# One core, trn2: the delta-rule stage of a two-layer decoder step written in another order

## Chip, cores, metric

One Trainium2 chip (trn2), one core. The metric is the device time of one call in microseconds (us), the median of three runs.

## The reference, cut to what matters

The program is one step of a decoder with two layers, over 256 prompt tokens and 8 sample tokens at once (T = 264 columns). Each layer adds four gated branches to x, then a mixture of experts. The change lies in the third branch, the gated delta rule with a state of 64 x 64 per head (4 heads):

```
qkv, conv_new = causal_conv(qkv_raw, conv0, w)        # 4 taps
qkv = silu(qkv);  gq, gk, gv = split(qkv)
gq = l2norm(gq) * 64 ** -0.5;  gk = l2norm(gk)
beta = sigmoid(b_raw)
g = -exp(a_log) * softplus(alpha_raw + dt_bias)
# per chunk, state s: 
gcum = cumsum(g);  decay = exp(tril(gcum_t - gcum_s))
lmat = eye + strict(beta * (k k^T) * decay)
u = solve(lmat, beta * v) - solve(lmat, beta * exp(gcum) * k) s
o = exp(gcum) * (q s) + ((q k^T) * decay) u
s = exp(g_last) * s + (exp(g_last - gcum) * u)^T k
c_out = rmsnorm(o) * silu(z_gate)
```

For the prompt s starts at zero; each of the 8 sample tokens has a state of its own and takes one step. The branch's gate is sigmoid of a column block of the input projection; there are 32 such blocks of 128 columns ("gate tiles") in a layer.

## The kernel before, in words

A layer is a chain of stages with a barrier of all engines behind each: `project`, `mla_prompt`, `mla_decode`, `gdn`, `memory`, `tail` (experts). All activations lie in on-chip memory with channels on partitions. Every engine has its own program, written by hand; semaphores order them, and an engine that waits holds up all that stands behind on it. There is no scheduler: the order in the code is the order on the engine.

The gate tiles are filler work for PE (TensorE). `gate_load` (L486) brings 512 KB of weights into one of two buffers `wf` on SP's DMA queue, `gate_multiply` (L494) runs 8 products of 128 x 128 by 264 columns on them, `gate_copy` (L507) takes the sum out of its PSUM bank on ACT. A load into a buffer waits until the product before it on that buffer is done. Before the change 8 tiles are multiplied in `mla_prompt`, 16 in `gdn`, 8 in `memory`.

`gdn` (L1297) handles the prompt as two chunks of 128 tokens (j = 0, 1). It has three parts.

- Head. DVE runs the convolution (L1558 to L1566), ACT its SiLU (L1510); DVE squares q and k (L1573), PE sums the squares per head with a block matrix (L1384), ACT takes four roots, DVE the reciprocal of 1,056 columns (L1582) and two multiplies (L1583, L1585). Then DVE and ACT make beta and the decay from short vectors of 12 columns (L1576 to L1599), DVE spreads them to `rep` (L1603), PE turns them into rows (L1400, L1402) and makes k k^T and k q^T (L1408), DVE the masked and decayed matrices AT, PT, MT (L1613 to L1625, once per chunk).
- Levels. The triangular inverse is made by doubling: after a level 0 (L1419) a loop of six levels, each with two products that hang on each other (L1426, then L1432 and L1435), ACT's copy between (L1539), and DVE's updates of X and XT (L1642, L1644). One gate tile stands at the end of each level.
- End. k and v are turned (L1444, L1448), the sample tokens' rows are spread, then per chunk: k s (L1464), q s (L1471), u (L1475), o (L1481), the new state (L1487), with DVE between them (L1700 to L1723). The sample tokens' state update (L1670 to L1733) stands between these DVE steps. Last the norm of o (L1728, L1498, L1548, L1736) and the product with the gate (L1737).

The first transfers that SP issues in `gdn` are the convolution's history `buf`, three small stores of runs of 12 or 32 bytes and the sample state; the stage's first gate load stands behind them.

## Time and profile before

| | us |
|---|---|
| three runs | 1571.75, 1576.78, 1569.12; median 1571.75 |
| profiled execution, its own time | 1580.17 |
| its span, first to last instruction | 1578.4 |
| PE busy in the span | 1331.3 (84%) |
| DVE, ACT, POOL busy | 722.7, 327.1, 183.0 |
| mean granted clock of PE | 0.92 of full |

The profile has one row for each group of instructions: when the group starts, how long it is busy, its engine and line, what it writes and reads, its count, and in brackets how long the engine stood idle before it and what ended that. PEclk in a window is the granted share of PE's full clock (1.00 is 2.4 GHz, 0.50 is 1.2 GHz). Matmuls in float32 have two records each. A row of windows has the stretch and its length, the busy time (and records) of PE, PEld (weight loads), DVE, ACT and POOL, then PEclk, the DMA engines' share and GB/s.

### The profile page before, as it was taken

How to read it: one execution, taken by the hardware profiler on the slowest of the kernel's cores; microseconds unless marked ns; L12 is line 12 of the kernel's file. 1: busy time of each engine (PE TensorE's matmuls, PEld its weight loads, DVE VectorE, ACT ScalarE, POOL GpSimd, SP SyncE). 2: the span in 40 equal slices, each digit the busy share in tenths (PEclk: the TensorE clock that was granted, in tenths of full speed). 3: DMA queues.
4: the chain of work that ended last, by engine and by line, in shares of the span. 5: the costliest groups of instructions: out<-in, count | busy, mean ns of one | idle time of the engine just before them, and what ended most of it. 6: DMA issues, size and time to landing. Idle time of an engine off the chain costs nothing. (4 is left out here: it accounts for less than half of the span.)

```text
span 1578.4 us, 23156 instructions
## 1 busy us (share of the span) xinstructions
PE 1331.3 (84%) x8264; PEld 921.3 (58%) x8264; DVE 722.7 (46%) x1485; ACT 327.1 (21%) x628; POOL 183.0 (12%) x192
## 2 busy tenths in 40 slices
PE   5988978977889799978779889789697897999876
PEld 3866756966466544433249666679564675444332
DVE  4664757365453512222246647463744525222222
ACT  0212613111121221111011235221102212121110
POOL 0050000000000243331000400000000003333210
PEclk9998989978899789999989989899798897899998
DMA  5372022126147189999734610311261482899995
GB/s 192 121 240 67 0 51 74 54 80 230 65 137 283 69 338 408 409 409 408 289 119 160 213 53 1 71 54 56 91 240 41 137 333 98 338 408 409 409 409 237
DMA packets 89962, 307.95 MB, mean 195 GB/s; under 512 B 16368, under 2 KB 19200, under 8 KB 88192
## 3 DMA queue, kind: packets, MB, share of 16 engines
q1 hardware_dynamic: 86784, 296.11, 50.1%
q0 software_dynamic: 3072, 10.49, 1.9%
q8 instruction: 59, 0.97, 0.3%
q14 instruction: 47, 0.39, 0.1%
HBM read 403.24 MB, written 3.98 MB: 258 GB/s over the span
## 5 line engine op out<-in xcount | busy, mean ns | idle before, releaser
L502 PE MATMUL bank<-hT,wf 128*128 128x264 f32 x1024 | 252.1, 405 | 34.4 <-PEq L205 19.5
L502 PEld LDWEIGHTS bank<-hT,wf 128*128 128x128 f32 x1024 | 202.4, 201 | 76.8 <-issue 23.0
L2032 PE MATMUL bank<-tail_wbase,tail_scr 128*32 128x512 f32 x1024 | 186.4, 604 | 21.2 <-DMA tail_wbase<-in_w_gu 21.2
L2032 PE MATMUL bank<-tail_wover,tail_scr 128*32 128x512 f32 x512 | 185.4, 601 | 4.5 <-DMA tail_wbase<-in_w_gu 4.5
L2366 DVE TENSOR_TENSOR xT<-xT,bank 128x264 f32<-128x264 f32 x192 | 73.7, 426 | 148.2 <-PE bank L2061 145.5
L2048 PE MATMUL bank<-tail_wbase,tail_acT 128*32 128x512 f32 x512 | 94.9, 622 | 22.2 <-DMA tail_wbase<-in_w_d 14.7
L2008 PEld LDWEIGHTS bank<-tail_G,tail_hTM 88*128 88x128 f32 x528 | 70.3, 196 | 68.5 <-issue 64.1
L2048 PE MATMUL bank<-tail_wover,tail_acT 128*32 128x512 f32 x256 | 94.6, 613 | 7.6 <-ACT tail_acT L2210 3.8
L1881 POOL MEMSET tail_wover<- 128x3072 f32 x2 | 5.3, 2659 | 805.5 <-PE bank L1970 805.5
L270 DVE TENSOR_TENSOR tail_Y<-bank,tail_Y 128x512 fp32r<-128x512 f32 x48 | 30.9, 686 | 146.1 <-ACT tail_Y L2215 146.1
L2008 PE MATMUL bank<-tail_G,tail_hTM 88*128 88x256 f32 x528 | 87.8, 305 | 2.8 <-ACT tail_scr L2160 2.8
L2032 PEld LDWEIGHTS bank<-tail_wbase,tail_scr 128*32 128x32 f32 x1024 | 42.6, 110 | 77.2 <-issue 73.2
L2160 ACT COPY tail_scr<-bank 128x256 f32<-128x256 f32 x96 | 35.8, 373 | 200.4 <-PE bank L2008 174.5
L1935 PE MATMUL bank<-brT,wbr 128*128 128x264 f32 x256 | 65.8, 420 | 9.7 <-DMA wbr<-in_w_br 5.2
L1911 POOL TENSOR_SCALAR tail_Gt<-tail_rows,cst 128x528 f32<-128x528 f32 x24 | 38.5, 1605 | 291.6 <-PE bank L2061 286.9
L1970 PE MATMUL bank<-hT,tail_wo 128*128 128x264 f32 x256 | 65.6, 408 | 4.7 <-DVE tail_last L2244 4.7
L2061 PE MATMUL bank<-tail_Q,tail_Y 128*128 128x264 f32 x384 | 65.5, 295 | 2.9 <-DVE tail_Y L270 2.8
L276 PE MATMUL bank<-proj_hsp,proj_wsp 128*128 128x264 f32 x224 | 64.6, 288 | 2.2 <-DVE proj_wsp L270 2.1
L1935 PEld LDWEIGHTS bank<-brT,wbr 128*128 128x128 f32 x256 | 52.5, 208 | 22.3 <-issue 12.2
L2061 PEld LDWEIGHTS bank<-tail_Q,tail_Y 128*128 128x128 f32 x384 | 53.8, 191 | 18.9 <-issue 11.7
L277 PE MATMUL bank<-proj_hsp,proj_wsp 128*128 128x264 f32 x224 | 63.5, 283 | 0.0
L278 PE MATMUL bank<-proj_hsp,proj_wsp 128*128 128x264 f32 x224 | 63.4, 283 | 0.0
(517 smaller groups left out, 2165.4 us busy)
## 6 DMA issues: line engine op xcount, KB each, us to landing
tail_wbase<-in_w_gu SPq DMA_DIRECT2D x256, 512.0 KB, 15.0
tail_wbase<-in_w_d SPq DMA_DIRECT2D x128, 512.0 KB, 15.1
tail_wover<-in_w_gu ACTq DMA_DIRECT2D x128, 512.0 KB
wf<-in_w_gate SPq DMA_DIRECT2D x64, 512.0 KB, 3.7
tail_wover<-in_w_d ACTq DMA_DIRECT2D x64, 512.0 KB
proj_wfm<-in_w_fm SPq DMA_DIRECT2D x28, 512.0 KB, 3.6
wbr<-in_w_br SPq DMA_DIRECT2D x16, 512.0 KB, 3.8
tail_wo<-in_w_out SPq DMA_DIRECT2D x16, 512.0 KB, 6.5
```

Source lines behind the costliest of these rows:

```text
L276: pe.matmul(out, wh, xh, start=start, stop=False)
L277: pe.matmul(out, wh, xl, start=False, stop=False)
L278: return pe.matmul(out, wl, xh, start=False, stop=stop)
L502: mm = pe.matmul(E["bank"][to][:, 0:T], F["wf"][slot][:, k, :], E["hT"][:, k, :], start=k == 0, stop=k == KT - 1)
L1911: nc.gpsimd.tensor_scalar(Gt[:], rows[:], C("slot")[:, q:q + 1], None, ALU.is_equal)\
L1935: mm = pe.matmul(bank[4 * s + b][:, 0:T], w[s][:, 2 * b + k, :], brT[:, 2 * b + k, :], start=k == 0, stop=k == 1)
L1970: mm = pe.matmul(bank[i][:, 0:T], wo[i][:, k, :], mixT[:, k, :], start=k == 0, stop=k == KT - 1)
L2008: mm = pe.matmul(bank[to][:, 0:GCOLS], h[0:n, c, P * k:P * k + P], G[g % 2][0:n, c, :], start=part == 0 and c == 0, stop=part == 1 and c == 2)
L2032: mm = pe.matmul(bank[0][W * p:W * p + W, :], HS[q // GROUP % 2][:, k, at + W * p:at + W * p + W], w[p][:, 512 * (k % 2):512 * (k % 2) + 5 ...
L2048: mm = pe.matmul(bank[2 + half][W * p:W * p + W, :], acT[:, f, W * p:W * p + W], w[p][:, 512 * half:512 * half + 512], start=f == 0, stop= ...
L2061: mm = pe.matmul(bank[4 + n % 3][:, 0:T], Y[part][:, P * d:P * d + P], Q[:, q % 2, :], start=part == 0, stop=part == 1)
L2366: tt(x, x, bank[4 + n % 3][:, 0:T], ALU.add).then_inc(S("x_ready"), 1)
```

## The change

- Gate tiles: tile 8 is multiplied in `mla_decode`, in front of the wait for the softmax's exponential, into PSUM bank 4, and kept in a new buffer `g8`; `gdn` copies it to its place and keeps 15 tiles. Of these, five stand in the head, one between level 0 and level 1, one behind each of levels 1 and 2, two behind each of levels 3, 4 and 5, none behind level 6, and the last one at the stage's very end.
- SP: the gate loads go first; the small stores are issued behind the load of the last gate tile. The last load for the next stage waits for the last gate product.
- Head: the short vectors of the decay come first on DVE; the convolution runs on four tiles (q, k), then the samples' taps as 4 instructions in place of 18, then on the other two; SiLU likewise in two pieces. The sums of squares go to 32 rows per tile, one root and one reciprocal of 264 columns stand for four; PE spreads the result with a selecting matrix `pick`, and DVE multiplies from PSUM.
- k and v are turned before level 0. Level 6 leaves out the update of X, which nobody reads.
- The steps of the sample state stand one after each level's MT on DVE (`between`).
- End: chunk 0 has no k s, q s and no decayed old state; the parts of o for chunk 1 add up in one bank; the norm of o is made in two halves.

```diff
-            for i in range(2):
-                gate_load(sp, S, A, l, F, i, MLA_TILES + i)
-            for i in range(2):
-                sp.wait_ge(S(f"gw{i}_loaded"), 16)
+            gate_load(sp, S, A, l, F, 0, MLA_TILES)
+            gate_load(sp, S, A, l, F, 1, MLA_TILES + 2)
+            gate_load(sp, S, A, l, F, 0, MLA_TILES + 1, used=1)
+            sp.wait_ge(S("gw0_loaded"), 32)
+            sp.wait_ge(S("gw1_loaded"), 16)
...
+            pe.wait_ge(S("rT_read"), 1)
+            gate_multiply(pe, S, E, F, 0, 1, 4)
             pe.wait_ge(S("exp_done"), 1)
...
+            pe.wait_ge(S("gate_copied"), 1)
             pe.transpose(bank[4][:, 0:P], lat[:], ident).then_inc(S("latT_done"), 1)
...
+            act.wait_ge(S("gate_done"), 1)
+            nc.scalar.copy(F["g8"][:], bank[4][:, 0:T]).then_inc(S("gate_copied"), 1)
...
         def _(sp):
             sp.dma_start(buf[:], A["sconv"][l]).then_inc(S("buf_loaded"), 16)
+            for r in range(2, 8):
+                gate_load(sp, S, A, l, F, r % 2, FIRST + r, used=r - 1)
+                if r == 3:
+                    sp.dma_start(st[:], A["sgdn"][l]).then_inc(S("state_loaded"), 16)
+            with sp.Fori(0, 3) as k:
+                for i in range(2):
+                    gate_load(sp, S, A, l, F, i, FIRST + 8 + i + 2 * k, used=2 * k + (7 + i))
+            sp.dma_start(F["memT"][:], A["memT"]).then_inc(S("mem_loaded"), 16)
+            gate_load(sp, S, A, l, F, 0, FIRST + 14, used=13)
+
             sp.dma_start(A["o_conv"][l], raw[:, :, NP_TOK - 3:NP_TOK]).then_inc(S("stored"), 16)
             sp.dma_start(A["o_convs"][l, :, :, 2, :], raw[:, :, NP_TOK:T]).then_inc(S("stored"), 16)
...
-            for r in range(2, 9):
-                gate_load(sp, S, A, l, F, r % 2, MLA_TILES + r, used=r - 1)
-            with sp.Fori(1, 7) as k:
-                gate_load(sp, S, A, l, F, 1, MLA_TILES + 8 + k, used=k + 8)
-            gate_load(sp, S, A, l, F, 0, MLA_TILES + 15, used=9)
-
-            sp.dma_start(F["memT"][:], A["memT"]).then_inc(S("mem_loaded"), 16)
-            gate_load(sp, S, A, l, F, 1, MLA_TILES + GDN_TILES + 1, used=15)
-            gate_load(sp, S, A, l, F, 0, MLA_TILES + GDN_TILES, used=16)
+            gate_load(sp, S, A, l, F, 1, MLA_TILES + GDN_TILES + 1, used=14)
             sp.wait_ge(S("state_s_ready"), 1)
             sp.dma_start(A["o_gdns"][l], st[:]).then_inc(S("stored"), 16)
-            sp.wait_ge(S("state_ready"), 8)
+            gate_load(sp, S, A, l, F, 0, MLA_TILES + GDN_TILES, used=15)
+            sp.wait_ge(S("state_ready"), 2)
...
-            for t in range(4):
-                mm = pe.matmul(bank[t][:, 0:T], C("blk"), sq[:, t, :], start=True, stop=True)
...
+            gates(0, 1, 2)
+            pe.wait_ge(S("sq_ready"), 1)
+            for t in range(4):
+                mm = pe.matmul(bank[2][32 * t:32 * t + 32, 0:T], C("blk")[:, 48:80], sq[:, t, :], start=True,
+                               stop=True)
+            mm.then_inc(S("ss_done"), 1)
+            gates(3)
+            pe.wait_ge(S("gb_ready"), 3)
...
+            pe.wait_ge(S("rinv_ready"), 1)
+            for t in range(4):
+                if t >= 2:
+                    pe.wait_ge(S("qk_ready"), t - 1)
+                pe.matmul(bank[2 + t % 2][:, 0:T], C("pick")[32 * t:32 * t + 32], rinv[32 * t:32 * t + 32, :],
+                          start=True, stop=True).then_inc(S("spread"), 1)
+            pe.wait_ge(S("rep_ready"), 4)
+            rows(0)
+            pe.wait_ge(S("qk_ready"), 4)
+            kq(0)
+            gates(4)
+            pe.wait_ge(S("G_ready"), 2)
+            rows(1)
+            pe.wait_ge(S("gate_copied"), 5)
+            kq(1)
+            pe.wait_ge(S("silu_done"), 2)
+            pe.wait_ge(S("bB_done"), 1)
+            turn(0)
+            level_zero(0)
+            pe.wait_ge(S("bB_done"), 2)
+            turn(1)
+            level_zero(1)
+            gate_multiply(pe, S, E, F, 1, 2, 7)
+            pe.wait_ge(S("kv_ready"), 2)
+            level(1)
+            gate_multiply(pe, S, E, F, 0, 3, 7, 6)
...
+            level(2)
+            gate_multiply(pe, S, E, F, 1, 3, 7, 7)
...
+            pe.wait_ge(S("rs_read"), 1)
+            with pe.Fori(3, LAST) as k:
+                level(k)
+                gate_multiply(pe, S, E, F, 0, k + 1, 7, 2 * k + 2)
+                gate_multiply(pe, S, E, F, 1, k + 1, 3, 2 * k + 2)
+            level(LAST, last=True)
+
+            pe.wait_ge(S("gate_copied"), 14)
+            pe.wait_ge(S("oX_ready"), 1)
+            for t in range(2):
+                mm = pe.matmul(bank[7][:, N * t:N * t + N], oX[:, 8 * t:8 * t + 8, :].rearrange("p a b -> p (a b)"),
+                               C("seln"), start=True, stop=True)
+            mm.then_inc(S("os_done"), 1)
+
...
+            pe.wait_ge(S("x0_ready"), 2 * LAST + 1)
+            values(0)
+            pe.wait_ge(S("x1_ready"), 2 * LAST + 1)
+            pe.wait_ge(S("us_ready"), 1)
+            state(0)
+            pe.wait_ge(S("u_ready"), 1)
...
+            pe.wait_ge(S("state_ready"), 1)
+            for h in range(H):
+                o, a = HD * (h % 2), h // 2
+                mm = pe.matmul(bank[h % 2][:, HD * a:HD * a + HD], y[o:o + HD, 2 + a, REST][:, 0:P],
+                               ST[o:o + HD, a, :], start=True, stop=True)
+            mm.then_inc(S("kS_done"), 1)
...
+                mm = pe.matmul(bank[4][:, P * t:P * t + P], C("blk"), osq[:, t, FIRST_HALF], start=True, stop=True)
+            mm.then_inc(S("oss_done"), 1)
+            values(1)
+            pe.wait_ge(S("u_ready"), 2)
...
+            pe.wait_ge(S("osq_ready"), 2)
+            n = T - P
             for t in range(2):
-                mm = pe.matmul(bank[t][:, 0:T], C("blk"), osq[:, t, :], start=True, stop=True)
+                mm = pe.matmul(bank[0][:, n * t:n * t + n], C("blk"), osq[:, t, REST], start=True, stop=True)
             mm.then_inc(S("oss_done"), 1)
+            gate_multiply(pe, S, E, F, 0, 7, 1)
...
+            nc.scalar.copy(F["gT"][:, 0, :], F["g8"][:])
+            gates(0, 1)
+            act.wait_ge(S("conv_ready"), 1)
+            nc.scalar.activation(y[:, 0:4, :], y[:, 0:4, :], ACT.Silu).then_inc(S("silu_done"), 1)
+            act.wait_ge(S("conv_ready"), 2)
+            nc.scalar.activation(y[:, 4:6, :], y[:, 4:6, :], ACT.Silu).then_inc(S("silu_done"), 1)
+            nc.scalar.activation(zg[:], zT[:, FM_ZG:FM_ZG + 2, :], ACT.Silu)
+            gates(2)
+            act.wait_ge(S("ss_done"), 1)
+            nc.scalar.activation(rinv[:], bank[2][:, 0:T], ACT.Sqrt, bias=eps).then_inc(S("root_ready"), 1)
+            gates(3)
...
+            nc.scalar.activation(sc1[:, 1:2], eps, ACT.Sqrt)
+            for k in (1, 2):
+                level(k)
...
+            taps((0, 1, 2, 3))
...
+            dve.wait_ge(S("buf_loaded"), 16)
+            past = pr[:].rearrange("p a b -> p (a b)")[:, 0:18 * N].rearrange("p (i t n) -> p i t n", i=3, t=6)
+            step(tt(past, buf[:].rearrange("p t i n -> p i t n"),
+                    V("conv", 0, 18).rearrange("p (i t) -> p i t", i=3).unsqueeze(3).to_broadcast([P, 3, 6, N]),
+                    ALU.mult))
...
+            taps((4, 5))
+
+            dve.wait_ge(S("silu_done"), 1)
+            step(tt(sq[:], y[:, 0:4, :], y[:, 0:4, :], ALU.mult), "sq_ready", wait=False)
...
+            dve.wait_ge(S("root_ready"), 1)
+            step(v.reciprocal(rinv[:], rinv[:]), "rinv_ready", wait=False)
             dve.wait_ge(S("G_done"), 1)
             for j in range(2):
                 step(v.tensor_copy(G[:, j], bank[4 + j][:, 0:H]), "G_ready")
+            for t in range(4):
+                dve.wait_ge(S("spread"), t + 1)
+                if t < 2:
+                    last = stt(y[:, t, :], y[:, t, :], HD ** -0.5, bank[2 + t % 2][:, 0:T], ALU.mult, ALU.mult)
+                else:
+                    last = tt(y[:, t, :], y[:, t, :], bank[2 + t % 2][:, 0:T], ALU.mult)
+                step(last, "qk_ready", wait=False)
...
+            between = (scaled_queries, sample_rows, sample_values, sample_new_value, sample_output, sample_state)
+            for k in range(1, LAST + 1):
+                for j in range(2):
+
+                    dve.wait_ge(S(f"p1{j}_done"), k)
+                    dve.wait_ge(S(f"x{j}_ready"), 2 * k)
+                    tt(MT[:, j], AT[:, j], C("lev", 7, P)[:, k:k + 1].to_broadcast([P, H, P]), ALU.mult)\
+                        .then_inc(S(f"mt{j}_ready"), 1)
+                between[k - 1]()
...
+                    dve.wait_ge(S(f"xp{j}_done"), k)
+                    if k < LAST:
+                        tt(X[:, j].rearrange("p h t -> p (h t)"), X[:, j].rearrange("p h t -> p (h t)"),
+                           bank[4 * j + 1][:], ALU.subtract).then_inc(S(f"x{j}_ready"), 1)
+                    tt(XT[:, j].rearrange("p h t -> p (h t)"), XT[:, j].rearrange("p h t -> p (h t)"),
+                       bank[4 * j + 2][:], ALU.subtract).then_inc(S(f"x{j}_ready"), 1)
...
+            dve.wait_ge(S("u_done"), 1)
+            decayed(0)
+            plain()
+            dve.wait_ge(S("ku_done"), 1)
+            step(v.tensor_copy(ST[:].rearrange("p a e -> p (a e)"), bank[6][:, 0:P]), "state_ready", wait=False)
+            dve.wait_ge(S("o_done"), 1)
+            step(v.tensor_copy(oT[:, :, FIRST_HALF], bank[5][:, 0:256].rearrange("p (a t) -> p a t", a=2)))
+            squares(FIRST_HALF)
+            dve.wait_ge(S("kS_done"), 1)
...
+            dve.wait_ge(S("oroot_ready"), 1)
+            step(v.reciprocal(osq[:, :, FIRST_HALF], osq[:, :, FIRST_HALF]), wait=False)
+            dve.wait_ge(S("o_done"), 2)
+            step(v.tensor_copy(oT[:, :, P:2 * P], bank[3][:, 0:256].rearrange("p (a t) -> p a t", a=2)))
+            squares(REST)
+            dve.wait_ge(S("osq_ready"), 2)
...
             dve.wait_ge(S("oroot_ready"), 2)
-            step(v.reciprocal(osq[:], osq[:]))
+            step(v.reciprocal(osq[:, :, REST], osq[:, :, REST]))
             step(tt(brT[:, 4:6, :], oT[:], osq[:], ALU.mult))
```

How the rows of the engines' programs lie (L502 before is L503 after, one line lower; L276 to L507 likewise). PE, from the stage's begin to the first products of level 0; before:

```order
L502 MATMUL bank<-hT,wf 128x264 x32
L1384 MATMUL bank<-gdn_sq,cst 128x264 x4
L502 MATMUL bank<-hT,wf 128x264 x32
L1389 MATMUL bank<-gdn_gb,cst 128x4 x2
L1400 MATMUL bank<-cst,gdn_rep 128x128 x4
L1402 MATMUL bank<-cst,gdn_rep 128x128 x4
L1408 MATMUL bank<-gdn_y 128x128 x8
L1400 MATMUL bank<-cst,gdn_rep 128x128 x4
L1402 MATMUL bank<-cst,gdn_rep 128x128 x4
L1408 MATMUL bank<-gdn_y 128x128 x8
L502 MATMUL bank<-hT,wf 128x264 x8
L1419 MATMUL bank<-cst,gdn_MT 128x128 x8
```

After the change:

```order
L503 MATMUL bank<-hT,wf 128x264 x24
L1443 MATMUL bank<-gdn_sq,cst 32x264 x4
L503 MATMUL bank<-hT,wf 128x264 x8
L1449 MATMUL bank<-gdn_gb,cst 128x4 x2
L1455 MATMUL bank<-gdn_rinv,cst 128x264 x4
L1397 MATMUL bank<-cst,gdn_rep 128x128 x4
L1399 MATMUL bank<-cst,gdn_rep 128x128 x4
L1407 MATMUL bank<-gdn_y 128x128 x8
L503 MATMUL bank<-hT,wf 128x264 x8
L1397 MATMUL bank<-cst,gdn_rep 128x128 x4
L1399 MATMUL bank<-cst,gdn_rep 128x128 x4
L1407 MATMUL bank<-gdn_y 128x128 x8
```

Three gate tiles (24 products), not four, stand in front of the sums of squares, one behind them, and one between the two chunks' rows; the squares' product has 32 rows of output, and four spreading products are new.

PE, one turn of the loop over the levels; before (P, X and XT are the inverse's pieces):

```order
L1426 MATMUL bank<-gdn_X,gdn_MT 128x128 x8
L1432 MATMUL bank<-gdn_P,gdn_XT 128x128 x4
L1435 MATMUL bank<-gdn_XT,gdn_P 128x128 x4
L1432 MATMUL bank<-gdn_P,gdn_XT 128x128 x4
L1435 MATMUL bank<-gdn_XT,gdn_P 128x128 x4
L498 ISA
L500 REGISTER_ALU
L502 MATMUL bank<-hT,wf 128x264 x8
```

After the change (levels 3 to 5):

```order
L1427 MATMUL bank<-gdn_X,gdn_MT 128x128 x8
L1433 MATMUL bank<-gdn_P,gdn_XT 128x128 x4
L1436 MATMUL bank<-gdn_XT,gdn_P 128x128 x4
L1433 MATMUL bank<-gdn_P,gdn_XT 128x128 x4
L1436 MATMUL bank<-gdn_XT,gdn_P 128x128 x4
L499 REGISTER_ALU
L501 REGISTER_ALU
L503 MATMUL bank<-hT,wf 128x264 x16
```

The loop's gate tile became two; it runs three times, where the one before ran six times.

SP, from the stage's begin, without the waits; before:

```order
L1349 DMA gdn_buf<-in_sconv 128x144
L1350 ISA
L1350 DMA o_conv<-zT 768x1x3
L1351 ISA
L1351 DMA o_convs<-zT 768x1x8
L1352 ISA
L1352 DMA gdn_st<-in_sgdn 128x1024
L1355 DMA o_convs<-gdn_buf 768x1x8
L1355 ISA
L1355 DMA o_convs<-gdn_buf 768x1x8
L491 ISA
L491 DMA wf<-in_w_gate 128x1024
```

After the change:

```order
L1361 DMA gdn_buf<-in_sconv 128x144
L492 ISA
L492 DMA wf<-in_w_gate 128x1024
L492 ISA
L492 DMA wf<-in_w_gate 128x1024
L1365 ISA
L1365 DMA gdn_st<-in_sgdn 128x1024
L492 ISA
L492 DMA wf<-in_w_gate 128x1024
```

Two gate loads stand where the stores stood.

## Rows read from the trace of the kernel before

**Rows 1.** Windows of `gdn`: layer 1, layer 2, layer 1's head, its levels

```profile
215.30:365.10 149.80, 121.36 (x747) 106.44 (x747) 90.39 (x192) 30.36 (x56) 0.00 (x0) 0.88 0.24 72
995.10:1147.30 152.20, 124.75 (x746) 108.79 (x746) 90.37 (x191) 30.36 (x56) 0.00 (x0) 0.86 0.24 71
215.30:275.60 60.30, 48.03 (x236) 39.97 (x236) 39.05 (x94) 17.50 (x32) 0.00 (x0) 0.92 0.31 81
275.60:327.50 51.90, 51.87 (x375) 49.08 (x376) 21.98 (x36) 8.93 (x17) 0.00 (x0) 1.00 0.22 74
```

**Rows 2.** DVE's timeline, layer 1, head and one level: start, us, line, bracket idle

```profile
217.03 7.43 DVE L1561 SCALAR_TENSOR_TENSOR gdn_y<-zT,vec,gdn_y 128x255 f32<-128x255 f32 x18
...
224.50 2.81 DVE L1566 SCALAR_TENSOR_TENSOR gdn_y<-gdn_buf,vec,gdn_y 128x8 f32<-128x8 f32 x18
...
237.78 1.26 DVE L1573 TENSOR_TENSOR gdn_sq<-gdn_y 128x1056 f32<-128x1056 f32 x1 [10.47 <-ACT gdn_y L1510]
...
242.88 6.75 DVE L1582 RECIPROCAL gdn_sq<-gdn_sq 128x1056 f32<-128x1056 f32 x1 [3.15 <-ACT gdn_sq L1515]
...
251.03 0.17 DVE L1587 TENSOR_SCALAR gdn_sp<-gdn_e 128x12 f32<-128x12 f32 x1
...
253.62 1.43 DVE L1603 COPY gdn_rep<-gdn_gb 128x512 f32<-128x512 f32 x4
...
259.93 0.69 DVE L1613 TENSOR_TENSOR gdn_D<-bank,gdn_G 128x512 f32<-128x512 f32 x1 [2.89 <-ACT gdn_EG L1526]
...
288.51 0.69 DVE L1642 TENSOR_TENSOR gdn_X<-gdn_X,bank 128x512 f32<-128x512 f32 x1 [4.69 <-PE bank L1435]
```

**Rows 3.** ACT's timeline, layer 1, the third gate tile's copy

```profile
234.54 0.38 ACT L511 COPY gT<-bank 128x264 f32<-128x264 f32 x1 [11.46 <-PE bank L502]
```

**Rows 4.** PE's timeline, layer 1, head and levels

```profile
227.97 10.09 PE L502 MATMUL bank<-hT,wf 128*128 128x264 f32 x32 [5.31 <-DMA wf<-in_w_gate]
...
281.13 3.73 PE L502 MATMUL bank<-hT,wf 128*128 128x264 f32 x16
...
284.69 1.95 PE L1426 MATMUL bank<-gdn_X,gdn_MT 128*128 128x128 f32 x16
...
290.10 3.73 PE L502 MATMUL bank<-hT,wf 128*128 128x264 f32 x16
```

**Rows 5.** PE's timeline, layer 1, chunk 1's first product at the end

```profile
345.21 1.12 PE L1464 MATMUL bank<-gdn_ST,gdn_y 64*128 64x64 f32 x8 [2.99 <-DVE gdn_ST L1723]
```

**Rows 6.** DVE's timeline, layer 1, the stage's last instruction

```profile
363.06 0.71 DVE L1737 TENSOR_TENSOR brT<-gdn_oT,gdn_osq 128x528 f32<-128x528 f32 x1
```

**Rows 7.** The gate loads (L491) of layer 1's `gdn`, issue to landing

```profile
DMA to landing us min/median/max: 3.3/3.4/8.3
```

**Rows 8.** PE's timeline, `mla_decode`, layer 1

```profile
203.39 1.97 PE L1180 MATMUL bank<-cst,mlad_sc 128*128 128x128 f32 x8 [3.23 <-ACT mlad_sc L1216]
```

**Rows 9.** DVE's timeline, `mla_decode`, layer 1, then layer 2

```profile
211.22 0.35 DVE L1287 SCALAR_TENSOR_TENSOR mlad_lat<-mlad_own,mlad_sc,bank 128x128 f32<-128x128 f32 x1 [2.54 <-PE bank L1187]
...
991.02 0.35 DVE L1287 SCALAR_TENSOR_TENSOR mlad_lat<-mlad_own,mlad_sc,bank 128x128 f32<-128x128 f32 x1 [1.03 <-PE bank L1187]
```

**Rows 10.** Windows for PEclk: a row of transposes twice, head, end, `memory`'s begin

```profile
151.00:155.00 4.00, 4.00 (x20) 4.00 (x20) 2.59 (x6) 1.17 (x2) 0.00 (x0) 0.50 0.28 110
155.00:160.00 5.00, 5.00 (x48) 5.00 (x47) 3.85 (x6) 3.22 (x6) 0.00 (x0) 1.00 0.00 0
270.70:275.60 4.90, 3.46 (x16) 3.17 (x16) 4.56 (x8) 0.00 (x0) 0.00 (x0) 0.65 0.14 58
345.00:365.00 20.00, 8.83 (x48) 6.89 (x48) 17.50 (x31) 0.85 (x2) 0.00 (x0) 0.50 0.08 29
365.00:371.00 6.00, 5.92 (x16) 4.71 (x17) 2.91 (x2) 0.00 (x0) 0.00 (x0) 0.58 0.81 294
```

**Rows 11.** PE's timeline, `mla_decode`, layer 1: products of 32 rows, then 128

```profile
190.53 1.92 PE L1163 MATMUL bank<-mlad_ckT,mlad_qblk 128*32 128x512 f32 x16
192.38 1.98 PE L1167 MATMUL bank<-mlad_krT,mlad_qrblk 128*128 128x512 f32 x4
```

359 lines of the change are left out of this document (161 added, 198 removed).

## Prediction, blind

> **What bounds the kernel now.** I read the windows of the stage first, since the mean over the kernel says nothing of a stage. In both layers `gdn` takes 150 us, with PE (TensorE) busy 121 to 125 and DVE (VectorE) 90 [rows 1]. Layer 1's stage falls into a head of 60.3 us, levels of 51.9 and an end of 149.8 - 60.3 - 51.9 = 37.6. The levels are PE's: busy 51.87 of 51.9 at full clock. Head and end are not: each is a chain through DVE, ACT (ScalarE) and PE, with the gate tiles as filler.
>
> The timelines show where the head's chain stands still. The convolution ends at 227.3 (224.50 + 2.81), 12.0 us into the stage, and DVE then idles 10.47 for ACT's SiLU [rows 2]. ACT has been idle for 11.46 in front of the third gate tile's copy, which stands ahead of the SiLU in its program [rows 3]; PE had waited 5.31 for that tile's weights [rows 4], because the load landed 8.3 us after its issue where the median is 3.4 [rows 7]. SP (SyncE) had put it behind the small stores. Next comes a reciprocal of 6.75 us, then a dozen short operations of 0.17, then the four copies to `rep` (1.43). Decay work on chunk 0 starts at 259.93 [rows 2], 44.6 us into the stage.
>
> **Head after the change.** DVE first does 8 short steps of the decay and the taps of the first four tiles: 8 x 0.2 (0.17 and a gap) + 1.7 for the first tap of all six tiles (217.03 - 215.30) + 12 of the 18 later taps at 7.43 / 18 = 0.41 + the samples' four steps, 0.85 by their columns: 9.2 us [rows 2]. The later taps of the last two tiles take 2.5 more (until 11.7) and cover the SiLU of the first four. No gate tile with a late load stands ahead of that SiLU now. The square (1.26) ends at 13.0. PE's four products with 32 rows of output come next: in `mla_decode` eight of them over 512 columns take 1.92, 0.24 each, where two with 128 rows take 1.98, 0.99 each [rows 11]. Four over 264 columns are thus bounded by 0.5 and 2.0; I take 0.5, of the same shape. The root (0.45) ends at 14.0; under it and behind it DVE makes the other short steps (1.7) and `rep` (1.4), until 16.1. The reciprocal of 264 columns, a quarter of 6.75, ends at 17.9. Four spreading products, 3.73 / 8 = 0.47 each [rows 4], alternate with four multiplies (0.43 each) until 20.8; the eight products on `rep`, priced as a level's first eight (1.95, 16 records [rows 4]), run from 20.0 to 22.0. After ACT's exponential of the row, 0.8 with its hand-overs, the decay of chunk 0 starts at 22.8 rather than 44.6.
>
> From there to level 1 it is 275.60 - 259.93 = 15.7 us now [rows 1, 2]. The change puts a gate tile (3.56) in between, and DVE's four writes of X and XT (some 2.5 at 0.6 to 0.69) come to lie under it: 16.8. So level 1 begins at 22.8 + 16.8 = 39.6, against 60.3. The head holds two stretches in which PE idles about 2 us (before the sums of squares and before chunk 1's level 0). Before, PE idled like this ahead of level 0, and the 4.90 us that followed ran at a granted 0.65 [rows 10]: that costs up to 4.90 x 0.35 = 1.7 us. I add 3.1 for two such dips: **42.7**.
>
> **Levels.** A level's own products take 290.10 - 281.13 - 3.56 = 5.41 (3.56: a tile's 3.73 less its overlap with what follows, 284.69 - 281.13) [rows 4]. Six of them less the left-out update (1.8), eight gate tiles of 3.56, the sample rows on PE (0.65 + 1.5, by their columns) and waits for copies at levels 1 and 3 (1.6) make 32.5 - 1.8 + 28.5 + 2.2 + 1.6 = **63.0**. DVE's sample steps, one group a level, I cost at nothing: DVE works 21.98 us in 51.9 of levels now [rows 1], and a gate tile or two cover a group of 1 to 3.5 us. Uncovered, they cost up to 14 us a layer (below).
>
> **End.** The products of chunk 0 with the old state go, and so does the sequence of sample steps. The new chain, product by product and DVE step by step (0.35 to 0.75 each, the reciprocals of 256 and 272 columns 1.7 to 1.8 by the row of 6.75), is an estimated 11 us at full clock. But now PE works with gaps, and the same place before ran 20 us at 0.50 with PE busy 8.83 [rows 10]; at half clock the chain's products, 5.5 us, would double, but some lie beside DVE's steps; I take 2.3 more: 13.3. Before, from chunk 1's first product to the last DVE step the end needed 363.77 - 345.21 = 18.6 [rows 5, 6]. Then something new closes the stage: the last gate tile, then the next stage's weights, whose load waits for that tile. At the next stage's begin one tile (16 records) takes 5.92 at a granted 0.58 [rows 10], so 5.9 (3.6 at full clock, 7.1 at half); a load 3.4 (bounds 3.3 and 8.3) [rows 7]; barrier 365.10 - 363.77 = 1.3. The norm of o and its product with the gate hide under these. Together 13.3 + 5.9 + 3.4 + 1.3 = **23.9**, against 37.6.
>
> The layer's sum is 42.7 + 63.0 + 23.9 = 129.6. Layer 1 gains 20.2, layer 2 (152.2) 22.6.
>
> **`mla_decode`.** The tile fills PE's wait of 3.23 for the exponential [rows 8] and outlasts it by about 0.5. In return the products behind it (1.97 now, after that wait) run at full clock, and DVE's wait of 2.54 at their end mostly goes; in layer 2 that wait is 1.03 [rows 9]. I take 1.9 and 0.5; bounds 0 and 3.6.
>
> **Stores.** SP issues the small stores behind the last gate load; two gate loads of 3.4 us fit a level of about 12.5. They end nothing, since the last weights land later.
>
> **Sum.** 20.2 + 22.6 + 1.9 + 0.5 = 45.2. The profiled execution took 1580.2, 0.5% above the median of the runs; 1580.2 - 45.2 = 1535.0, times 1571.75 / 1580.17, is **1527 us**.
>
> **Bounds.** Best: no dip and full clock to the end, 42.7 - 3.1 + 63.0 + (11 + 3.6 + 3.4 + 1.3) = 121.9 a layer, a gain of 60.6 with `mla_decode`: 1511. Worst within this account: the last tile at 7.1, its load at 8.3 and nothing in `mla_decode`: 135.7 a layer, a gain of 30.6: 1541.
>
> **A rule against the change.** Each chunk's k and v are now turned just ahead of its level 0. Where a row of transposes ran in `mla_decode`, its first 4 us were granted 0.50 and the next 5.00 us, 48 records of transposes and nothing else, 1.00 [rows 10]: the clock rose under transposes, so I charge nothing for them. The Trainium skill, "TensorE: Matmul & The Clock Gate", section "Part 4: PE-mode transpose", says that a transpose does not count as PE work for the clock in the way a product does, and that the full clock does not engage on it. By that rule the turns would hold the clock at half into level 1. In rows of this case that is gate tile 5 at 7.1 for 3.6 and part of level 1's 5.41 twice over, about 5 us a layer: 1527 + 10 = 1537. The trace disagrees with it; it keeps a chance of 0.03.
>
> **Rivals.**
> - *The clock stays full* through head and end: 1511, chance 0.09. For it, the gate tiles are better spread; against it, the end still has gaps, and gaps cost the clock in the old end [rows 10].
> - *The close of the stage costs more*: a late load, the last tile at half clock and a longer chain of o. 1541, and up to 1556 if half of the 14 us of sample steps shows as well: 0.10.
> - *Sample steps stand in the way, and the change brings nothing.* They come on DVE between MT and the updates that PE needs for its next level. DVE's work outside head and levels is 90.39 - 39.05 - 21.98 = 29.4 us [rows 1], of which I count about 14 as sample steps. If none is covered, 14 a layer, on top of the worst end: 30.6 - 28 leaves 3, no change, 1569. Against it, DVE waits 4.69 for PE ahead of its update in a level with one gate tile [rows 2]. Chance 0.05.
> - *Slower: half clock in the levels.* Two gaps of 2 us precede them, more waits stand between them, and in `mla_decode` a gap of 3.23 was followed by products at half clock, 1.97 for eight records, where a level's sixteen take 1.95 [rows 4, 8]. If the clock fell at level 1 and stayed at 1.2 GHz, 62.8 us of PE work a layer would double: 125.6 - 45.2 = 80 slower, 1652. It decides from 45.2 / 125.6 = 36% of the levels at half. Against it: a gate tile or two stand in every level but the last, and behind the dip ahead of level 1 the levels before were granted 1.00 throughout [rows 1, 10]. Chance 0.03.
>
> **Numbers.** The account above keeps 0.70, with a range of its own from 1511 to 1541; 0.03 for 1537, 0.09 at 1511, 0.10 up to 1556, 0.05 no change, 0.03 slower. A measurement of this kernel tells about 0.5% (8 us) from nothing. All but the last two are faster by more: 0.92, 0.05, 0.03. The range from 1511 to 1546 leaves out those two and the far part of the costly close.
>
> **What would show it.** In layer 1 of the changed profile: square started 12 us into the stage; decay of chunk 0 at 23; first product of level 1 at 40 to 43; PEclk 1.00 in the levels and about two dips in the head; two tiles a level with a period of 12.5; the last gate tile begun 118 to 120 us in, and a stage of 130; `mla_decode`'s waits of 2.54 and 1.03 gone. I am wrong if DVE ends PE's waits at levels 3 to 5, if PEclk stays at half behind the turns, or if the last load lands later than 4 us after its issue.

## The result, and the profile after

Four runs of the changed kernel took 1510.26 to 1524.50 us, median 1520.53; four of the kernel before 1569.12 to 1576.78, median 1573.70. The ratio is 0.9657 (95% interval 0.9617 to 0.9697): 53 us shorter, where 45 were forecast. Two later groups of runs of the same changed kernel gave 0.9719 (0.9675 to 0.9763) and 0.9643 (0.9606 to 0.9679).

The windows of the changed kernel, with the columns of [rows 1]: the stage in layer 1, in layer 2, then layer 1's head, levels and end.

```profile
208.31:335.25 126.94, 111.38 (x717) 96.89 (x717) 74.79 (x162) 28.18 (x54) 0.00 (x0) 0.95 0.29 81
956.29:1083.76 127.47, 113.51 (x716) 98.60 (x717) 74.88 (x161) 28.26 (x54) 0.00 (x0) 0.94 0.29 81
208.31:249.69 41.38, 35.70 (x204) 29.36 (x205) 32.72 (x86) 15.14 (x28) 0.00 (x0) 0.96 0.24 79
249.69:313.38 63.69, 62.30 (x422) 56.79 (x420) 31.34 (x55) 11.70 (x23) 0.00 (x0) 1.00 0.33 85
313.38:335.25 21.87, 13.38 (x95) 10.73 (x93) 10.72 (x22) 1.34 (x3) 0.00 (x0) 0.77 0.29 74
```

The stage takes 126.94 and 127.47 us for 149.80 and 152.20. The head is 41.4 for 60.3, the levels 63.7 with eight gate tiles for 51.9 with six, the end 21.9 for 37.6. PE is busy 62.30 of the 63.69 us of the levels at a granted 1.00; the end has 0.77.

TensorE's timeline in the head:

```profile
221.40 0.66 PE L1443 MATMUL bank<-gdn_sq,cst 128*32 128x264 f32 x8 [1.76 <-DVE gdn_sq L1663]
...
221.99 5.52 PE L503 MATMUL bank<-hT,wf 128*128 128x264 f32 x16
...
229.08 1.04 PE L1455 MATMUL bank<-gdn_rinv,cst 32*128 32x264 f32 x4 [0.59 <-DVE gdn_y L1686]
...
246.13 3.73 PE L503 MATMUL bank<-hT,wf 128*128 128x264 f32 x16
```

VectorE's, for the rows of [rows 2]:

```profile
220.09 1.25 DVE L1663 TENSOR_TENSOR gdn_sq<-gdn_y 128x1056 f32<-128x1056 f32 x1
...
224.30 1.80 DVE L1679 RECIPROCAL gdn_rinv<-gdn_rinv 128x264 f32<-128x264 f32 x1
...
232.77 0.69 DVE L1694 TENSOR_TENSOR gdn_D<-bank,gdn_G 128x512 f32<-128x512 f32 x1 [2.18 <-ACT gdn_EG L1589]
```

The square starts 11.8 us into the stage (22.5 before, after an idle of 10.47), and the decay of chunk 0 24.5 us in (44.6 before). The reciprocal is 1.80 for 6.75. PE idles 1.76 ahead of the sums of squares, and the tile behind that gap takes 5.52 where a tile takes 3.83 at full clock: a dip, as a stretch at half clock is called below. Tile 5, behind a gap of 3.19 ahead of chunk 1's level 0, takes 3.73: no dip here.

TensorE in the levels: the one wait on a sample step, and a pair of tiles.

```profile
272.08 2.05 PE L1427 MATMUL bank<-gdn_X,gdn_MT 128*128 128x128 f32 x16 [0.72 <-DVE gdn_rs L1750]
...
277.58 7.29 PE L503 MATMUL bank<-hT,wf 128*128 128x264 f32 x32
```

All that VectorE's sample steps cost in the levels of this profile is this wait of 0.72 us, ahead of level 3; beside it stand their products on TensorE. TensorE in the end, and the next stage's first product:

```profile
322.73 1.28 PE L1554 MATMUL bank<-gdn_osq,cst 128*128 128x136 f32 x4 [1.96 <-DVE gdn_osq L1808]
...
323.80 6.12 PE L503 MATMUL bank<-hT,wf 128*128 128x264 f32 x16
...
335.25 9.15 PE L503 MATMUL bank<-hT,wf 128*128 128x264 f32 x32 [5.32 <-PEq L206]
```

The last tile begins 115.5 us into the stage and takes 6.12, at a granted 0.60. The load that waits for it lands 3.6 us after its issue, and the next stage starts 5.32 after the tile's end.

In `mla_decode` of layer 1 (TensorE, then VectorE's row that answers to [rows 9]):

```profile
195.62 3.72 PE L503 MATMUL bank<-hT,wf 128*128 128x264 f32 x16
...
199.18 1.04 PE L1184 MATMUL bank<-cst,mlad_sc 128*128 128x128 f32 x8
...
200.36 3.70 PE L1191 MATMUL bank<-mla_ck,mla_kr 128*32 128x128 f32 x128
```

```profile
204.21 0.35 DVE L1294 SCALAR_TENSOR_TENSOR mlad_lat<-mlad_own,mlad_sc,bank 128x128 f32<-128x128 f32 x1 [0.26 <-PE bank L1191]
```

The eight transposes behind the wait (a transpose has one record here, where a product has two) take 1.04 for the 1.97 of [rows 8], and VectorE's wait of 2.54 is 0.26.

**What the two profiles don't share.** Their spans differ by 70.0 us (1578.4 and 1508.4), far more than the medians. The stage and `mla_decode` of both layers account for 50.9; 19.1 lie in stages whose code is the same. One profile was the slowest, the other the fastest execution of its kernel. So in all that follows a part is judged by the length of its stage.

### The profile page after: what moved, and what is told of

Same layout as the page of the kernel before. It is cut to its first block and busy times, and to the rows that moved or that the text cites. A ratio compares the mean times of both kernels' runs of the same rounds, so it can differ in the third digit from the quotient of the medians.

```text
span 1508.4 us, 22910 instructions
## 1 busy us (share of the span) xinstructions
PE 1303.5 (86%) x8236; PEld 897.5 (60%) x8236; DVE 690.5 (46%) x1425; ACT 323.6 (21%) x626; POOL 182.9 (12%) x192
## 5 line engine op out<-in xcount | busy, mean ns | idle before, releaser
L503 PE MATMUL bank<-hT,wf 128*128 128x264 f32 x1024 | 253.5, 407 | 17.5 <-PEq L206 16.9
L503 PEld LDWEIGHTS bank<-hT,wf 128*128 128x128 f32 x1024 | 203.4, 202 | 60.7 <-issue 21.6
L2155 PE MATMUL bank<-tail_wbase,tail_acT 128*32 128x512 f32 x512 | 95.2, 625 | 21.9 <-DMA tail_wbase<-in_w_d 14.5
L2042 PE MATMUL bank<-brT,wbr 128*128 128x264 f32 x256 | 62.7, 406 | 7.5 <-PEq L206 4.5
```

Source lines behind the costliest of these rows:

```text
L503: mm = pe.matmul(E["bank"][to][:, 0:T], F["wf"][slot][:, k, :], E["hT"][:, k, :], start=k == 0, stop=k == KT - 1)
L2042: mm = pe.matmul(bank[4 * s + b][:, 0:T], w[s][:, 2 * b + k, :], brT[:, 2 * b + k, :], start=k == 0, stop=k == 1)
L2155: mm = pe.matmul(bank[2 + half][W * p:W * p + W, :], acT[:, f, W * p:W * p + W], w[p][:, 512 * half:512 * half + 512], start=f == 0, stop= ...
```

## The experiments

The table has each profile's stage lengths, from the first instruction of a stage to that of the next; "other" is the span less these four; "level 1" is when level 1's first product starts in the stage, "decay" when VectorE starts the decay of chunk 0 (layer 1, layer 2). The first two rows are one group of runs; e0 to e3, then e4, e5, e9 and e10, then e8, e11 and e12, then e7 are four more, each with its own runs of the kernel before. Medians compare within a group, ratios across groups.

| kernel | `mla_decode` | `gdn` | decay | level 1 | other | median of runs | ratio to before (95%) |
|---|---|---|---|---|---|---|---|
| before | 68.8, 67.8 | 149.8, 152.2 | 44.6, 45.8 | 60.3, 61.4 | 1139.8 | 1573.7 | |
| changed | 66.8, 66.5 | 126.9, 127.5 | 24.5, 24.1 | 41.4, 43.2 | 1120.7 | 1520.5 | 0.9657 (0.9617 to 0.9697) |
| e0_again | 66.6, 66.8 | 127.5, 130.1 | 24.2, 24.5 | 43.2, 43.1 | 1129.3 | 1527.3 | 0.9719 (0.9675 to 0.9763) |
| e12_again | 66.5, 66.7 | 130.2, 130.2 | 24.5, 23.8 | 43.1, 43.0 | 1126.5 | 1516.8 | 0.9643 (0.9606 to 0.9679) |
| e1_no_tile | 67.8, 67.5 | 127.1, 125.3 | 24.4, 22.9 | 43.0, 39.8 | 1137.8 | 1528.5 | 0.9704 (0.9648 to 0.9759) |
| e2_stores_first | 66.8, 66.4 | 131.3, 127.9 | 28.5, 25.3 | 47.1, 43.9 | 1121.4 | 1523.4 | 0.9700 (0.9652 to 0.9747) |
| e10_silu_behind | 66.8, 66.5 | 138.2, 140.3 | 35.1, 34.6 | 53.7, 53.2 | 1123.6 | 1541.0 | 0.9835 (0.9795 to 0.9875) |
| e4_wide_norms | 66.7, 66.7 | 131.5, 131.5 | 25.2, 25.2 | 47.3, 47.4 | 1131.2 | 1525.8 | 0.9722 (0.9689 to 0.9755) |
| e5_decay_late | 67.0, 66.7 | 133.7, 133.6 | 27.5, 27.5 | 46.6, 46.6 | 1131.4 | 1532.8 | 0.9760 (0.9713 to 0.9806) |
| e9_wide_and_late | 66.6, 66.5 | 136.8, 136.6 | 33.3, 33.3 | 51.1, 51.0 | 1128.4 | 1537.8 | 0.9795 (0.9752 to 0.9837) |
| e3_late_samples | 66.9, 66.7 | 136.6, 136.3 | 24.5, 22.9 | 43.1, 41.2 | 1135.0 | 1541.5 | 0.9787 (0.9742 to 0.9833) |
| e7_last_tile | 66.6, 66.6 | 124.8, 121.3 | 24.5, 22.9 | 43.1, 41.2 | 1121.7 | 1509.7 | 0.9617 (0.9587 to 0.9646) |
| e8_both | 66.8, 66.6 | 123.6, 123.5 | 25.5, 25.5 | 41.1, 41.0 | 1128.8 | 1509.6 | 0.9599 (0.9564 to 0.9634) |
| e11_rows_early | 66.5, 66.6 | 124.2, 124.1 | 26.9, 26.9 | 43.2, 43.3 | 1122.4 | 1506.5 | 0.9579 (0.9543 to 0.9615) |

The three profiles of the changed kernel give six lengths of `gdn`, 126.9 to 130.2, mean 128.7: the measure below.

**The changed kernel again (e0_again, e12_again).** No edit.

> The changed kernel itself, once more. The two profiles so far differ by 70.0 us in span: 50.9 us of it lie in mla_decode and gdn of both layers, 19.1 us in stages whose code is the same. Theory A: those 19.1 are the spread between executions (one profile was the slowest, the other the fastest of its kernel's runs). Then the stages with the same code take anything from 1121 to 1140 us in this profile, while gdn comes back at 127 us in each layer within 1 us and mla_decode at 66.5 to 67; time 1510 to 1526. Theory B: the change also shortens the other stages, by the state it leaves. Then they take 1121 us again, within 3.

> The changed kernel a third time, as the measure for the two others of this group. gdn 127 to 130 us in each layer, with the level 1 product 41.4 to 43.2 us into it and 20 to 21 us from the levels to the next stage; 1510 to 1530 us. Both theories of the other two runs say the same of it.

The stages with the same code took 1129.3 and 1126.5 us; over all profiles they range from 1120.7 to 1139.8. Theory B (1121 within 3) falls; most of the 19.1 us is the spread between executions. Theory A was too narrow for the stage: `gdn` came back at 127.5 and 130.1, where it had 127 within 1, and e0_again's median is 1527.3, where it had 1510 to 1526. Whether the kernel before also has a few us more there on the mean, one profile of it can't tell. In `gdn` the spread is the clock's. TensorE in layer 1 of e12_again:

```profile
227.09 5.51 PE L503 MATMUL bank<-hT,wf 128*128 128x264 f32 x16
...
251.24 5.41 PE L503 MATMUL bank<-hT,wf 128*128 128x264 f32 x16
...
278.98 3.58 PE L1427 MATMUL bank<-gdn_X,gdn_MT 128*128 128x128 f32 x16 [0.82 <-DVE gdn_rs L1750]
```

Here both tile 3 and tile 5 ran partly at half clock, 1.7 us each, and so did level 3's first products, behind the wait for the sample step (3.58 for 2.05). This last dip is in three of the six layers, in both of e12_again and in layer 2 of e0_again (3.67), and makes their levels 1.6 us longer. Nor does the head's first dip always fall on tile 3. In three of the six layers (layer 2 of the first profile and of e12_again, layer 1 of e0_again) tile 3 took 3.83 and products behind it ran at half clock, in two of them with an idle of only 0.2 ahead of the sums. TensorE in layer 1 of e0_again (the last two rows take 1.16 and 1.06 at full clock):

```profile
223.54 0.65 PE L1443 MATMUL bank<-gdn_sq,cst 128*32 128x264 f32 x8 [0.24 <-DVE gdn_sq L1663]
224.13 3.83 PE L503 MATMUL bank<-hT,wf 128*128 128x264 f32 x16
...
230.58 1.57 PE L1397 MATMUL bank<-cst,gdn_rep 128*128 128x128 f32 x8
231.94 1.92 PE L1399 MATMUL bank<-cst,gdn_rep 128*128 128x128 f32 x8
```

**The tile in `mla_decode` (e1_no_tile).**

```diff
-            gate_multiply(pe, S, E, F, 0, 1, 4)
+            pe.matmul(bank[4][:, 0:8], F["wf"][0][:, 0, :], E["hT"][:, 0, 0:8], start=True, stop=True)\
+                .then_inc(S("gate_done"), 1)
```

> Of gate tile 8's product in mla_decode a single small product is left (8 columns of one of its eight), so that PE idles through the wait for the exponential as it did before the change; the tile's value is left out. Theory A: the tile's worth in mla_decode is the clock it keeps. With less work to do, mla_decode gets longer: by 1.5 to 2 us in layer 1 (to 68.3 to 68.8) and by about 1.3 in layer 2, and the products behind the wait run at half clock (four transposes 1.97 us for 1.04); gdn is unchanged. About +3 us in all against the changed kernel. Rival: the tile is only work in a gap. Then mla_decode stays within 0.3 us or gets shorter by the 0.5 us that the tile outlasts the wait.

TensorE in layer 2, behind the wait for the exponential (layer 1 has the same 1.97, behind 3.10):

```profile
964.04 1.97 PE L1186 MATMUL bank<-cst,mlad_sc 128*128 128x128 f32 x8 [3.10 <-ACT mlad_sc L1223]
...
965.94 4.17 PE L1193 MATMUL bank<-mla_ck,mla_kr 128*32 128x128 f32 x128
```

With 3.6 us of work fewer, `mla_decode` was 1.2 and 0.8 us longer than in the changed kernel's profiles (67.80, 67.46 against means of 66.63 and 66.67), and the transposes ran at half clock. The rival falls; theory A has the sign and the mechanism, and a price that was half again too high (2.0 in all for about 3). The run's median shows no difference: 2 us can't be seen in it.

**Stores first (e2_stores_first).** The small stores and the sample state go back in front of the third gate load.

```diff
+            sp.dma_start(A["o_conv"][l], raw[:, :, NP_TOK - 3:NP_TOK]).then_inc(S("stored"), 16)
+            sp.dma_start(A["o_convs"][l, :, :, 2, :], raw[:, :, NP_TOK:T]).then_inc(S("stored"), 16)
+            sp.dma_start(st[:], A["sgdn"][l]).then_inc(S("state_loaded"), 16)
...
             for r in range(2, 8):
                 gate_load(sp, S, A, l, F, r % 2, FIRST + r, used=r - 1)
```

> SyncE issues the small stores and the sample state in front of the third gate load again, as before the change; all else as changed. Theory A: the third gate tile's weights land about 12.7 us into the stage (its load is issued 4.3 us in and takes 8.3), so PE idles about 5 us ahead of tile 2, which then runs partly at half clock; the sums of squares start near 18 us into the stage (13.1 as changed), and gdn gets 3 to 5.5 us longer in each layer: +6 to +11 us for the kernel. Rival: the convolution sets the head's pace and PE's filler has room; gdn grows by less than 1 us a layer.

TensorE's third gate tile, layer 1 and layer 2:

```profile
223.69 6.36 PE L503 MATMUL bank<-hT,wf 128*128 128x264 f32 x16 [5.14 <-DMA wf<-in_w_gate]
...
974.09 3.83 PE L503 MATMUL bank<-hT,wf 128*128 128x264 f32 x16 [2.79 <-DMA wf<-in_w_gate]
```

In layer 1 the wait of [rows 4] is back (5.14 for 5.31), the third tile takes 6.36, the decay starts 4.2 later than the mean of 24.2, and the stage has 131.3, 2.6 more than 128.7. In layer 2 the load was long too: it landed 6.1 us after its issue, against 8.1 in layer 1 and 3.4 to 3.5 in the changed kernel. In the stage that is 11.8 us in, against 12.5. But the first two tiles took 9.04 there for 7.36, so that TensorE idled only 2.79, and the third tile behind that ran at full clock (3.83). Of the 3.2 us between the two layers' decays 0.7 is the load's and 2.5 the clock's. Layer 2's head is 1.1 longer than the mean and its stage not at all. So theory A has the mechanism in layer 1, with less in the stage than its 3 to 5.5, and the rival has layer 2; the clock behind the wait makes the difference. The runs' median shows no loss (1523.4; e0_again, in the same group, 1527.3).

**SiLU behind the tile's copy too (e10_silu_behind).** As above, and:

```diff
-            gates(0, 1)
+            gates(0, 1, 2)
             act.wait_ge(S("conv_ready"), 1)
...
-            gates(2)
             act.wait_ge(S("ss_done"), 1)
```

> The small stores are issued ahead of the third gate load again, and ScalarE's copy of the third gate tile stands ahead of its SiLU, as before the change; all else as changed. The single change of the stores moved the decay of chunk 0 by 4 us in layer 1 and 1 in layer 2. Theory A (the late load reaches VectorE through that copy): the square starts 18 to 21 us into the stage in place of 11.8, and gdn grows by 6 to 9 us a layer. Rival (the copy's place is nothing by itself): as with the stores alone, +4 in layer 1 and +1 in layer 2.

ScalarE's copy of the third tile, then VectorE's square, layer 1:

```profile
230.00 0.38 ACT L512 COPY gT<-bank 128x264 f32<-128x264 f32 x1 [11.15 <-PE bank L503]
```

```profile
232.81 1.26 DVE L1661 TENSOR_TENSOR gdn_sq<-gdn_y 128x1056 f32<-128x1056 f32 x1 [9.87 <-ACT gdn_y L1578]
```

These are [rows 3] and the second row of [rows 2] again: 11.15 and 9.87 idle for 11.46 and 10.47. The square starts 21.7 and 21.0 us in, and the stage is 9.5 and 11.6 longer than 128.7, above theory A's 9. The rival falls: a filler's copy in front of a chain's step hands that chain the filler's load. What the copy's place costs with an early load was not run.

**Norms and decay (e4_wide_norms, e5_decay_late, e9_wide_and_late).** In the first the four sums, roots, the reciprocal of 1,056 columns and two multiplies are back; in the second the decay's short vectors stand behind the multiplies; in the third both.

```diff
-            nc.scalar.activation(rinv[:], bank[2][:, 0:T], ACT.Sqrt, bias=eps).then_inc(S("root_ready"), 1)
+            for t in range(4):
+                nc.scalar.activation(sq[:, t, :], bank[t][:, 0:T], ACT.Sqrt, bias=eps).then_inc(S("root_ready"), 1)
...
-            step(v.reciprocal(rinv[:], rinv[:]), "rinv_ready", wait=False)
+            step(v.reciprocal(sq[:], sq[:]))
```

The second, on ScalarE (its two other engines likewise):

```diff
-            act.wait_ge(S("neg_ready"), 2)
-            nc.scalar.activation(e1[:], e1[:], ACT.Exp, scale=-1.0).then_inc(S("e1_done"), 1)
...
             gates(3)
+            act.wait_ge(S("neg_ready"), 2)
+            nc.scalar.activation(e1[:], e1[:], ACT.Exp, scale=-1.0).then_inc(S("e1_done"), 1)
```

> The norms of q and k are wide again (four sums of 128 rows, four roots, one reciprocal of 1,056 columns, two multiplies; no spreading products); all else as changed. By the rows of the changed kernel the square ends 13.0 us into the stage, the sums take 2.0, the roots 1.6 to 1.9, the reciprocal 6.75, the multiplies 1.4 and the copy of G 0.4. Theory A (the short reciprocal is paid back by the spreading products and the four multiplies, and the decay chain covers the rest): the decay of chunk 0 starts 0.5 to 2 us later than now (24.1 to 24.5 into the stage), gdn grows by 0.5 to 2 us a layer, 1 to 4 in all. Theory B (the prediction's: the reciprocal's 5 us are gained on the path): gdn grows by about 5 us a layer, +10 in all.

> The short vectors of the decay stand behind the norms' multiplies again, on VectorE, ScalarE and TensorE; the norms stay compact. Theory A (two chains side by side, each covers the other): the decay of chunk 0 starts 1 to 3 us later than now, gdn +1 to +3 us a layer. Theory B (the decay's steps, 3.3 + 1.7 + 1.4 us and two table loads of 1.28 are each gained on the path by coming early): gdn +6 to +9 us a layer.

> Both at once: wide norms and the decay's short vectors behind them, as before the change; loads, SiLU and all behind the head as changed. Theory A: the two chains now stand one behind the other, and the cost is more than the sum of the two single ones: the decay of chunk 0 starts 6 to 9 us later than in the changed kernel (near 31), gdn +6 to +9 us a layer. Theory B (costs add): the sum of the two single ones, within 1 us.

Against the means of the six (decay at 24.2, level 1 at 42.8), with wide norms the decay starts only 1.0 us later, as theory A had it; but level 1 comes 4.5 later and the stage is 2.8 longer, between the theories (these two layers have no dip at level 3, and the end is 1.0 shorter than the mean). TensorE and VectorE in e4_wide_norms tell why:

```profile
235.96 2.24 PE L1407 MATMUL bank<-gdn_y 64*128 64x128 f32 x16 [4.04 <-DVE gdn_y L1676]
...
238.13 5.86 PE L503 MATMUL bank<-hT,wf 128*128 128x264 f32 x16
```

```profile
246.52 0.69 DVE L1684 TENSOR_TENSOR gdn_D<-bank,gdn_G 128x512 f32<-128x512 f32 x1 [4.80 <-ACT gdn_EG L1584]
```

TensorE waits 4.04 for the normed q and k in front of the products k q^T, and these (1.26 at full clock) and part of the tile behind them (3.83) run at half. Chunk 1's rows stand behind that tile, so VectorE idles 4.80 for their exponential. With the decay late, the same happens one step earlier (TensorE in e5_decay_late):

```profile
229.79 1.01 PE L1455 MATMUL bank<-gdn_gb,cst 128*128 128x4 f32 x4 [3.19 <-DVE gdn_gb L1680]
...
231.26 2.08 PE L1397 MATMUL bank<-cst,gdn_rep 128*128 128x128 f32 x8 [0.45 <-DVE gdn_rep L1684]
```

The decay starts 3.2 later, the stage is 5.0 longer: above theory A's 3, below theory B's 6. With both, VectorE and TensorE in e9_wide_and_late:

```profile
227.65 6.75 DVE L1654 RECIPROCAL gdn_sq<-gdn_sq 128x1056 f32<-128x1056 f32 x1 [3.15 <-ACT gdn_sq L1575]
...
243.99 0.69 DVE L1683 TENSOR_TENSOR gdn_D<-bank,gdn_G 128x512 f32<-128x512 f32 x1 [4.31 <-ACT gdn_EG L1584]
```

```profile
238.09 0.99 PE L1449 MATMUL bank<-gdn_gb,cst 128*128 128x4 f32 x4 [8.62 <-DVE gdn_gb L1670]
```

Now the reciprocal and the decay stand one behind the other and TensorE waits 8.62. For the start of the decay theory A holds: 9.1 later, where the single ones give 1.0 + 3.2. For the stage theory B holds: 8.0 longer, where they give 2.8 + 5.0. Each single undoing already left TensorE idle, and paid at chunk 1 and in the clock what it saved at chunk 0.

**Sample steps behind the levels (e3_late_samples).** All but the first group and the prompt's beta v leave the loop; their products on TensorE stand behind the levels too.

```diff
-            between = (scaled_queries, sample_rows, sample_values, sample_new_value, sample_output, sample_state)
+            between = (scaled_queries, prompt_values)
...
             decayed(1)
+            sample_values()
+            sample_new_value()
+            sample_output()
             dve.wait_ge(S("oroot_ready"), 1)
```

> The sample state's steps stand behind the levels again, between the end's steps (their three groups of products on PE too), all else as changed. Theory A: in the levels they cost only the 0.7 us that PE waits ahead of level 3; in the end their 10 us of DVE lie on the path from the values of o to the norm, so gdn gets 8 to 11 us longer in each layer, +16 to +22 us in all. Rival: the last gate tile and its load close the stage, and DVE idles in the end anyway, so that the steps hide there: less than 3 us a layer.

TensorE in the end, then VectorE's first and last sample step ahead of the norm:

```profile
330.91 1.02 PE L1547 MATMUL bank<-cst,gdn_oX 128*128 128x8 f32 x4 [7.25 <-DVE gdn_oX L1770]
...
334.66 1.27 PE L1553 MATMUL bank<-gdn_osq,cst 128*128 128x136 f32 x4 [2.73 <-DVE gdn_osq L1808]
...
347.77 2.54 PE L503 MATMUL bank<-hT,wf 128*128 128x264 f32 x5 [7.14 <-PEq L206]
```

```profile
323.45 1.23 DVE L1753 TENSOR_TENSOR gdn_pr<-gdn_st,gdn_rs 128x1024 f32<-128x1024 f32 x1
...
330.43 0.42 DVE L1770 TENSOR_TENSOR gdn_oX<-cst,gdn_v 128x256 f32<-128x256 f32 x1
```

The steps stand on the path from 323.06 to 332 and TensorE waits 7.25 for them. The stage is 7.8 longer (136.5 for 128.7), the levels 3.7 shorter in layer 1 (60.9 for 64.6, to the last write of XT): the wait of 0.72 and the two groups of products, which now stand behind. So 7.8 is a difference: the end alone, from the last product of the levels to the next stage, grew by 12.9 (33.3 and 34.9 for a mean of 21.3), and the levels and, by a dip fewer in layer 2, the head gave 5.1 back. The rival falls; theory A's 8 was just missed, and in the runs the kernel was 14 us slower in its group (medians 1541.5 and 1527.3), not 16.

**Tiles moved into the gaps (e8_both, e11_rows_early, e7_last_tile).**

```diff
-            gates(0, 1, 2)
+            gates(0, 1, 2, 3)
             pe.wait_ge(S("sq_ready"), 1)
...
-            level_zero(1)
-            gate_multiply(pe, S, E, F, 1, 2, 7)
+            gate_multiply(pe, S, E, F, 1, 2, 3)
+            level_zero(1)
...
             state(1)
+            gate_multiply(pe, S, E, F, 0, 7, 1)
             pe.wait_ge(S("osq_ready"), 2)
```

The first has all three, the last only the third. The second has besides:

```diff
             kq(0)
-            gates(4)
             pe.wait_ge(S("G_ready"), 2)
             rows(1)
+            gates(4)
```

> The changed kernel with three gate tiles put where TensorE idles: tile 3 in front of the sums of squares, tile 5 in front of level 0 of chunk 1, the last tile in front of the second half's sums of squares in the end. Theory A (PE's gaps of 1.8, 3.2 and 2.0 us are paid for by the half clock behind them, and the last tile and its load close the stage): level 1 comes 38.5 to 41 us into the stage (41.4 to 43.2 now), the levels' end is followed by the next stage after 15.5 to 17 us (20 to 21 now), gdn is 119 to 123 us; 12 to 17 us off the whole. Rival (each tile now stands on the path in front of a norm: the sums wait 1.9 to 3.5 us for tile 3, the second root 3.6 for the last): what the tile gives at its old place it takes at the new; gdn within 2 us of 128.

> The same three moves, and the rows of chunk 1's decay ahead of gate tile 4 in place of behind it. Theory A (VectorE idles 1.3 us for chunk 1's exponential now, since the rows stand behind a tile): level 1 comes 0.8 to 1.4 us earlier still, gdn 118 to 122; some 2 us of the whole. Rival (the tile's copy on ScalarE now stands between chunk 1's two exponentials and holds the second): no gain, within 0.4 us of the run with the three moves alone.

> Of the three moves only the last: the last gate tile in front of the second half's sums of squares, in TensorE's gap in the end; the head as changed. Theory A (the whole gain of the three moves, 5 to 6 us a layer, came from the end; in the head the gap only went elsewhere): the levels' end is followed by the next stage after 15.5 us (20 to 21 now), level 1 comes 41.4 to 43.2 us into the stage, gdn takes 121.5 to 125 us, 10 to 12 us off the whole, and the time is that of the three moves together within its uncertainty. Rival (tile 5's move in the head gave part of it): gdn stays at 125 to 127.

TensorE in e8_both:

```profile
234.09 1.25 PE L1454 MATMUL bank<-gdn_rinv,cst 32*128 32x264 f32 x4 [1.90 <-DVE gdn_rinv L1679]
...
237.44 2.08 PE L1397 MATMUL bank<-cst,gdn_rep 128*128 128x128 f32 x8
...
257.20 3.33 PE L1427 MATMUL bank<-gdn_X,gdn_MT 128*128 128x128 f32 x16 [1.92 <-DVE gdn_MT L1784]
...
330.66 3.83 PE L503 MATMUL bank<-hT,wf 128*128 128x264 f32 x16
...
334.32 0.63 PE L1554 MATMUL bank<-gdn_osq,cst 128*128 128x136 f32 x4
...
339.75 5.62 PE L503 MATMUL bank<-hT,wf 128*128 128x264 f32 x17 [4.81 <-PEq L206]
```

In the end theory A holds: the last tile takes 3.83 at full clock, the sums behind it 0.63, and the next stage starts 15.5 us after the levels for 20 to 21. In the head the rival holds. TensorE no longer idles ahead of the sums, but a gap of 1.9 us turns up ahead of the spreading products and again ahead of level 1, with half clock behind it (2.08 for the 1.16 of the rows, 3.33 for the 1.95 of a level's first products). The stage has 123.5 us, 5.2 less than 128.7 and just outside theory A's 119 to 123. The end gives 5.0 of it; what the head gains (level 1 at 41.0 for 42.8) the levels lose (66.3 for 64.6). The median is 7.3 below e12_again's in the same group, where theory A had 12 to 17. e7_last_tile, with the end's move alone, confirms the end: 124.8 and 121.3 us, mean 123.1, its ends 5.0 shorter than the mean too, and a ratio of 0.9617 for 0.9599, the same within the intervals. The rows ahead of tile 4 gave nothing: from the decay to level 1 it is 16.3 us for e8_both's 15.5. TensorE in e11_rows_early waits for tile 4's copy on ScalarE, as the rival said. That the decay itself starts 1.4 later there is not the edit's: the first four tiles, ahead of the sums, took 16.6 us in both layers for 14.9.

```profile
244.50 1.26 PE L1407 MATMUL bank<-gdn_y 64*128 64x128 f32 x16 [0.47 <-ACT gT L512]
```

Its median, 1506.5, is the lowest, but its stage is 0.6 longer than e8_both's, and its stages with the same code are shorter (1122.4 and 1128.8 in the profiles). All runs of e8_both and e11_rows_early (1502.4 to 1511.2) are below those of e12_again in their group (1512.4 to 1522.0). For e7_last_tile the runs can't say as much, since its interval (0.9587 to 0.9646) overlaps two of the changed kernel's three; there the stage's length tells. The edit that pays is the last tile's.

## Why the prediction was right, and where its steps were off

- **Head, 42.7 us:** measured 41.4 in layer 1 of the first profile and 43.0 to 43.2 in the changed kernel's five other layers. Its steps hold up to the end of the square, 13.0 us into the stage. The root ends at 15.1 and not at 14.0, for ScalarE's table load of 1.28 stands ahead of it; but the reciprocal waits for `rep` and ends at 17.8 (forecast 17.9). In layer 1 of the first profile the decay of chunk 0 starts at 24.5 and not at 22.8, because tile 3 fell to half clock behind the gap of 1.76 and holds up G and the spreading products. That dip was in the sum, but as a lump behind the chain. Without a dip the working comes out: in layer 2 of e1_no_tile, whose head is the changed kernel's, the clock stayed full through the head from the third tile on, the decay starts at 22.9 and level 1 at 39.8 (forecast 22.8 and 39.6). Two dips came, as forecast, in five of the six layers, one in the sixth.
- **What made the head shorter:** the reading of [rows 2 to 4] stands, and is the largest part: stores and SiLU put back cost 10.5 us a layer, norms and decay together 8.0. The working priced the reciprocal as a cut of 6.75 to 1.8 on the path. Alone it is worth 1.0 at the start of the decay; it reaches the stage through TensorE's wait for q and k.
- **Levels, 63.0:** measured 63.7 in the first profile, from level 1's first product to the first behind the levels. VectorE's sample steps, priced at nothing, took 0.72, and in three of six layers 1.6 more by the dip behind that wait. So one of the signs that were to prove the prediction wrong did come, that VectorE ends a wait of TensorE at levels 3 to 5; it cost 0.7 to 2.3 us and not 14. The 14 for uncovered steps fit: put into the end, where nothing covers them, they and their products make it 12.9 longer.
- **End, 23.9:** measured 21.9 (20.6 to 21.8 in the other five layers). The chain was 10.4 at a granted 0.90, and not 13.3: the clock fell only at the last gap. The last tile at 6.12 (5.9 forecast) and the close at 5.3 (4.7) were as told.
- **`mla_decode`, 1.9 + 0.5:** the profiles show 2.0 to 2.3 and 1.1 to 1.3. e1_no_tile gives 1.2 and 0.8 of it to the tile's clock. In layer 1 the products behind the transposes took 5.77 in the kernel before and 4.29 in e1_no_tile, with the same wait ahead; why, and so what the rest is, stays open, with one profile each.
- **The sum:** the forecast of 45.2 stands against 302.0 - 257.5 = 44.5 in `gdn` (means) and 136.6 - 133.3 = 3.3 in `mla_decode`, 47.8. The three ratios give 44 to 56 us. That the stage's sum came so near is in part luck: the end was 2 to 3 us shorter than forecast, the levels 0.7 to 2.3 longer.
- **The rule against the change.** In the changed kernel's first profile the turns of chunk 1 stand 4 to 6 us ahead of tile 5, which ran at 3.73, full clock, in layer 1; in the five other layers it took 5.4. TensorE had idled 3.2 us between in all six, so these rows can't tell. In e8_both tile 5 stands right behind the turns (TensorE, layer 1; layer 2 has 3.73 too):

```profile
250.23 0.60 PE L1413 MATMUL bank<-cst,gdn_y 128*128 128x128 f32 x4
250.66 3.73 PE L503 MATMUL bank<-hT,wf 128*128 128x264 f32 x16
```

It ran at full clock, 1.00 granted through the turns and the tile. The Trainium skill, "TensorE: Matmul & The Clock Gate", section "Part 4: PE-mode transpose", has the full clock not engage on transposes. These rows show no loss behind the turns.

- **Slower at half clock in the levels:** in the changed kernel's six layers the levels ran at 1.00, but for level 3's first products in three of them.

Of the stage's 22.3 us the undoings name 10.5 (load and SiLU), 8.0 (norms and decay) and 7.8 (sample steps), and one gate tile, 3.6, went to `mla_decode`: 29.9. The close by a tile and its load, new here, takes some of that back (5.0 by e7_last_tile's end). What chunk 0 without state terms and the norm in halves gave was not run by itself; it is in the remainder, which is too small against a spread of 3 us to be told.

## What to carry to other kernels

Ask of each filler which chain its bookkeeping touches: the copy of a tile's result in front of a chain's step on another engine made a late weight load cost 10 us a layer, and the load alone 2.6 in one layer and nothing in the other. A shorter step off the longest chain may still pay, or not, by the wait that it leaves on the engine with the clock; price the gap, and what runs behind it. And don't let the last filler and the load that waits for it close a stage: moved forward by one group of products, into a gap of 2 us, it gave 5 us a layer.

## What the runs showed of the hardware

- The same gap did not always cost the clock. Behind the 3.2 us ahead of chunk 1's level 0, tile 5 took 3.73 us in one layer of the changed kernel's three profiles and 5.40 to 5.42 in the five others. Behind 1.75 to 1.86 ahead of the sums, tile 3 took 5.51 or 5.52 in three layers, and behind 1.71 it took 3.83 (layer 2 of e12_again). The clock also fell where TensorE had idled no more than 0.6 us at a time since the stage began: the row at 231.94 in e0_again above. So one kernel's stage varies from 126.9 to 130.2 us without an edit, its head by 1.8, its levels by 1.6, its end by 1.2. What decides it stays open.
- Stages with the same code differed by up to 19 us in sum between executions (1120.7 to 1139.8).
- The load behind the small stores took long in all six layers that have it ahead of the third tile: it landed 8.3 and 8.5 us after its issue before, 8.1 and 6.1 in e2_stores_first, 8.1 and 7.0 in e10_silu_behind. With no store ahead of it the third tile's load took 3.4 to 3.5 in the changed kernel's six layers. There the stores stand ahead of a load near the levels' end, which took 6.8 to 8.8 and which nothing waited for.
